# A two-block transformer kernel on one core: context work spread over the last feed-forward, retention decay arguments computed there, and another order of the expert down products

## The reference: what is computed

```
def first_block(x, ...):
    for l in range(2):
        x = x + 0.5 * swiglu(rms_norm(x, g0), ffn_w_gate[l, 0], ffn_w_up[l, 0], ffn_w_down[l, 0])   # 1024 -> 2816 -> 1024
        h = rms_norm(x, g1)
        ...                                      # three kinds of attention, gated and merged
        x = x + merged @ w_o[l]
        x = x + 0.5 * swiglu(rms_norm(x, g2), ffn_w_gate[l, 1], ffn_w_up[l, 1], ffn_w_down[l, 1])
    return rms_norm(x, final_g)

def second_block(x, c, ctx, c_ctx, ...):
    mod_x = silu(c) @ w_ada + b_ada              # shifts, scales and gates for x
    mod_c = silu(c_ctx) @ w_ada + b_ada          # the same for the context
    hx = _rmsnorm(x, norm1_g) * (1 + sc1) + sh1
    hc = _rmsnorm(ctx, norm1_g) * (1 + csc1) + csh1
    qa, ka, va, qr, kr, vr, gr = split(hx @ w_in)            # of hc: ka, va, kr, vr
    attn_x = softmax attention of x over context and x
    ret_x  = retention: scores times exp(log_g * distance), forward and backward
    x = x + gt1 * (concat(attn_x, ret_x) @ w_out)
    h2 = _rmsnorm(x, norm2_g) * (1 + sc2) + sh2
    logits = h2 @ w_router + b                   # 4 groups and 32 experts
    x = x + gt2 * (two chosen experts: (silu(h2 @ w_gate[e]) * (h2 @ w_up[e])) @ w_down[e])
    return _rmsnorm(x, final_norm_g)
```

## Time and profile before

| | |
|---|---|
| median of 3 runs | 1986.72 us (1986.06 to 1990.2) |
| the profiled execution | 1989.03 us |
| its span | 1987.1 us |
| TensorE busy | 1936.6 us (97%) |
| VectorE busy | 1236.4 us (62%) |
| ScalarE busy | 702.0 us (35%) |
| mean granted TensorE clock | 0.992 of 2.4 GHz |

### The profile page before, as it was taken

How to read it: one execution, slowest core, us unless ns; L and a number is a source line. 1 busy time by engine, 2 the same in 40 slices (tenths; PEclk the granted TensorE clock), 3 DMA queues, 4 the chain that set the end, 5 groups by cost and what they waited for, 6 DMA issues and landing times.

```text
span 1987.1 us, 33458 instructions
## 1 busy us (share of the span) xinstructions
PE 1936.6 (97%) x13957; PEld 1594.9 (80%) x13957; DVE 1236.4 (62%) x2117; ACT 702.0 (35%) x1046; POOL 40.5 (2%) x28
## 2 busy tenths in 40 slices
PE   9999999999999999999999999999899999999997
PEld 9999998889999999999888999999566444433432
DVE  7665759877567877785987777767766332222221
ACT  5433436535334533443653544343332000000001
POOL 1000100001000100010000100000000000000000
PEclk9999999999999999999999999999899999999999
DMA  8798563276776677666325675654309999999996
GB/s 246 246 357 252 176 184 114 96 212 207 220 221 203 210 233 228 201 184 185 117 96 179 204 239 185 201 121 128 127 22 369 402 421 421 421 421 422 421 421 280
DMA packets 275425, 476.64 MB, mean 240 GB/s; under 512 B 29270, under 2 KB 235152, under 8 KB 250696
## 3 DMA queue, kind: packets, MB, share of 16 engines
q1 hardware_dynamic: 275020, 474.38, 68.8%
q10 hardware_dynamic: 252, 0.08, 0.0%
HBM read 473.27 MB, written 7.95 MB: 242 GB/s over the span
## 4 chain that ended last, share of the span: by engine, by line
PE 82%; DMA 8%; DVE 6%; ACT 2%; SPq 1%; issue 1%; DVEq 0%; ACTq 0%
PE ps L793 81%; DMA ring_over<-in_moe_w_up_dram 3%; DMA ring_zone<-in_moe_w_up_dram 3%; DMA hl_place<-in_moe_w_up_dram 1%; DMA ring_over<-in_moe_w_gate_dram 1%; SPq L713 1%; PE ps L1121 1%; DVE WL L1900 1%; ACT mT L1546 0%; DVE hl L1912 0%; DVE xT L1919 0%; PE ps L1264 0%; DVE PT L2348 0%; DVE WL L1972 0%; PE ps L1441 0%
## 5 line engine op out<-in xcount | busy, mean ns | idle before, releaser
L793 PE MATMUL ps<-hh,WH 128*128 128x256 f32 x2232 | 633.3, 284 | 6.2 <-DVE WL L1900 5.6
L1900 DVE SCALAR_TENSOR_TENSOR WL<-W,WH 128x1024 fp32r<-128x1024 f32 x390 | 484.6, 1257 | 232.6 <-ACT WH L1523 231.0
L793 PE MATMUL ps<-hl,WH 128*128 128x256 f32 x2232 | 622.7, 279 | 0.0
L793 PE MATMUL ps<-hh,WL 128*128 128x256 f32 x2232 | 622.6, 279 | 0.0
L1523 ACT ACTIVATE WH<-W 128x1024 fp32r<-128x1024 f32 x390 | 408.6, 1056 | 432.9 <-PE ps L793 406.4
L793 PEld LDWEIGHTS ps<-hh,WH 128*128 128x128 f32 x2232 | 418.9, 188 | 18.1 <-issue 15.0
L793 PEld LDWEIGHTS ps<-hl,WH 128*128 128x128 f32 x2232 | 418.4, 187 | 1.2 <-issue 1.0
L793 PEld LDWEIGHTS ps<-hh,WL 128*128 128x128 f32 x2232 | 419.1, 188 | 0.0
L793 PE MATMUL ps<-hid_h,WH 128*128 128x256 f32 x704 | 200.9, 285 | 0.0
L793 PE MATMUL ps<-hid_l,WH 128*128 128x256 f32 x704 | 197.5, 280 | 0.0
L793 PE MATMUL ps<-hid_h,WL 128*128 128x256 f32 x704 | 197.4, 280 | 0.0
(11 more groups left out here) (407 smaller groups left out, 2618.0 us busy)
## 6 DMA issues: line engine op xcount, KB each, us to landing
W<-in_ffn_w_gate_dram SPq DMA_DIRECT2D x88, 512.0 KB, 4.8
W<-in_ffn_w_up_dram SPq DMA_DIRECT2D x88, 512.0 KB, 4.8
W<-in_ffn_w_down_dram SPq DMA_DIRECT2D x88, 512.0 KB, 3.8
W<-in_w_in_dram SPq DMA_DIRECT2D x78, 512.0 KB, 4.4
ring_over<-in_moe_w_gate_dram SPq DMA_DIRECT2D x29, 1024.0 KB, 25.3
ring_over<-in_moe_w_up_dram SPq DMA_DIRECT2D x28, 1024.0 KB, 24.5
W<-in_w_gate_dram SPq DMA_DIRECT2D x48, 512.0 KB, 3.5
ring_zone<-in_moe_w_down_dram SPq DMA_DIRECT2D x24, 1024.0 KB, 26.3
```

What stands on the lines that cost most here:

```text
L793: ins = nc.tensor.matmul(o, lhsT, rhs, start=start, stop=stop, skip_group_check=True, **kw)
L1900: v.scalar_tensor_tensor(out=low, in0=W[:, i % RAW, :], scalar=1.0, in1=high.bitcast(F32), op0=ALU.mult, op1=ALU.subtract).then_inc(low_re ...
```

## The change

The change has three parts.

1. The context's work in block 6 is broken up. The product of the shift and the router's weights, and VectorE's copy of its row, go to block 7 (`router_shift`, `shift_row`); the spreading matmul and `LB` go from block 7 to block 8. In block 6 VectorE and ScalarE now issue one split behind the second group of the context (`used(1)` at b == 1), and count one less at the block's end.
2. The decay arguments of the four heads are computed by VectorE at the ends of blocks 7, 8, 9 and 10 of the last feed-forward, with scratch in `QK[:, 16:18]`. In the input product only exponentials and sums are left, and `tmpD` has four tiles, one a head. ScalarE waits for argument h + 1 of `dpart`.
3. In `down_product` the second half of the chunks (j = 1) is done half of the columns by half: both chunks for columns 0 to 511, then both for 512 to 1023.

```diff
-        tmpD = flat(mT[:, :, :])[:, 0:512]
+        tmpD = [flat(mT[:, :, :])[:, h * 512:(h + 1) * 512] for h in range(4)]
+        arg_part = flat(QK[:, 16:18, :])
...
                     turns.step()
+
+            def router_shift():
+
                 bank = begin()
                 for k in range(KD):
                     mm(bank[0:1, 0:40], MOD[:, 24 + k, 0:1], WR[:, k, :], k == 0, k == KD - 1,
...
                     if (l, i, b) == (1, 1, CONTEXT_AT + 2):
+                        router_shift()
+                    if (l, i, b) == (1, 1, CONTEXT_AT + 3):
                         pe.wait_ge(lrow_ready, 1)
...
                 for j in range(2):
                     w = [take("moe_down") for e in range(2)]
-                    for c in (2 * j, 2 * j + 1):
-                        for half in range(2):
-                            at = (c % 2) * D + half * 512
-                            for e in range(2):
+                    turn = [(c, half) for c in (2 * j, 2 * j + 1) for half in range(2)]
+                    if j:
+                        turn.sort(key=lambda ch: ch[1])
+                    for c, half in turn:
+                        at = (c % 2) * D + half * 512
+                        for e in range(2):
...
                     nc.scalar.activation(hc_h[:, 2 * b:2 * b + 2, :], cT[:, 2 * b:2 * b + 2, :], ACT.Copy)\
                         .then_inc(ctx_high, 1)
                     turns.step()
+                    if b == 1:
+                        used(1)
...
                     if b:
-                        used(2)
+                        used(1 if (l, i, b) == (1, 1, CONTEXT_AT + 1) else 2)
...
-                act.wait_ge(dpart, due(dpart))
+                act.wait_ge(dpart, h + 1)
...
+            def decay_arg(h):
+
+                own = Dm[:, h, 2:4, :].rearrange("p a t -> p (a t)")
+                v.tensor_scalar(own, const("distance"), 0.0, lf[:, h:h + 1], ALU.max, ALU.mult)
+                link(v.tensor_scalar(arg_part, const("distance"), 0.0, dect[:, 4 + h:5 + h], ALU.min, ALU.mult))
+                v.tensor_tensor(own, own, arg_part, ALU.add).then_inc(dpart, 1)
+                dve.wait_ge(dpart, h + 1)
...
                         v.tensor_tensor(hc_l[:, 2 * b - 2:2 * b, :], cT[:, 2 * b - 2:2 * b, :],
                                         hc_h[:, 2 * b - 2:2 * b, :].bitcast(F32), ALU.subtract).then_inc(ctx_low, 1)
+                    if b == 1:
+                        used(1)
+
+            def shift_row():
+
                 bank = take()
                 give(v.tensor_copy(lrow[:, :], bank[0:1, 0:40]))
...
+                    if (l, i) == (1, 1) and CONTEXT_AT + 2 <= b < CONTEXT_AT + 6:
+                        decay_arg(b - CONTEXT_AT - 2)
...
                 if 0 < p - DECAY_AT <= 4:
                     decay_sum(p - DECAY_AT - 1)
-                if 0 <= p - DECAY_AT < 4:
-                    decay_arg(p - DECAY_AT)
```

More of the change, by code:

```diff
@@ L1452, in down_product @@
                     w = [take("moe_down") for e in range(2)]
-                    for c in (2 * j, 2 * j + 1):
-                        for half in range(2):
-                            at = (c % 2) * D + half * 512
-                            for e in range(2):
-                                mm(bank[half][e * SLOTS:(e + 1) * SLOTS, :], hidT[:, c, e * SLOTS:(e + 1) * SLOTS],
-                                   w[e][:, at:at + 512], c == 0, c == HIDDEN - 1,
-                                   then=work_ready if e and c == HIDDEN - 1 else None)
+                    turn = [(c, half) for c in (2 * j, 2 * j + 1) for half in range(2)]
[4 more added lines that the diff above has]
+                        for e in range(2):
+                            mm(bank[half][e * SLOTS:(e + 1) * SLOTS, :], hidT[:, c, e * SLOTS:(e + 1) * SLOTS],
+                               w[e][:, at:at + 512], c == 0, c == HIDDEN - 1,
+                               then=work_ready if e and c == HIDDEN - 1 else None)
                     done_plain(2)
@@ L1641, in ffn @@
                         round_context()
-                        turns.step()
-                    if (l, i, b) == (1, 1, CONTEXT_AT + 2):
-                        turns.step()
+                    turns.step((l, i, b) in ((1, 1, CONTEXT_AT + 2), (1, 1, CONTEXT_AT + 3)))
                     if b:
-                        used(2)
+                        used(1 if (l, i, b) == (1, 1, CONTEXT_AT + 1) else 2)
                 turns.step(ada_unit(l, i, FF_BLOCKS - 1) is not None)
@@ L1748, in decay @@
                 dist = const("distance").rearrange("p (a t) -> p a t", a=2)
-                act.wait_ge(dpart, due(dpart))
+                act.wait_ge(dpart, h + 1)
                 nc.scalar.activation(ctxd, dist, ACT.Exp, bias=lf256[:, h:h + 1], scale=lf[:, h:h + 1])
-                nc.scalar.activation(tmpD.rearrange("p (a t) -> p a t", a=2), dist, ACT.Exp,
+                nc.scalar.activation(tmpD[h].rearrange("p (a t) -> p a t", a=2), dist, ACT.Exp,
                                      bias=lf256[:, 4 + h:5 + h], scale=dect[:, 4 + h:5 + h])
@@ L2174, in ffn @@
                     if (l, i, b) == (1, 1, CONTEXT_AT + 2):
+                        shift_row()
+                    if (l, i, b) == (1, 1, CONTEXT_AT + 3):
                         bank = take()
@@ L2371, in side @@
                     both(5, 7, QK[:, 5, :])
-            def decay_arg(h):
-                own = Dm[:, h, 2:4, :].rearrange("p a t -> p (a t)")
-                v.tensor_scalar(own, const("distance"), 0.0, lf[:, h:h + 1], ALU.max, ALU.mult)
-                link(v.tensor_scalar(PT[:, 0, :], const("distance"), 0.0, dect[:, 4 + h:5 + h], ALU.min, ALU.mult))
-                v.tensor_tensor(own, own, PT[:, 0, :], ALU.add).then_inc(dpart, 1)
             def decay_sum(h):
@@ L2381, in decay_sum @@
                 ctxd = Dm[:, h, 0:2, :].rearrange("p a t -> p (a t)")
-                link(v.tensor_tensor(ctxd, ctxd, tmpD, ALU.add))
+                link(v.tensor_tensor(ctxd, ctxd, tmpD[h], ALU.add))
             for p, g in enumerate(ORDER):
```

## The result

| | before | after |
|---|---|---|
| median, runs side by side | 1988.46 us (1986.06 to 1990.56, 4 runs) | 1969.49 us (1968.79 to 1971.52, 4 runs) |
| ratio | | 0.991, 95% interval 0.9894 to 0.9926 |
| the profiled execution | 1989.03 us | 1971.52 us |
| its span | 1987.1 us | 1969.7 us |
| TensorE busy | 1936.6 us (97%) | 1927.9 us (98%) |

The time lies 0.1 us from the predicted 1969.4 us, inside the range. Part of so small a distance is luck, as the experiments show. The profiled execution became 17.5 us shorter; the sum had 17.3.

A forecast was written before the change was run, and what follows sets the result against it. TensorE, holding 82% of the chain of waits, was taken as the bound, with waits behind VectorE; loads bound the experts' stage. Savings of 5.1 + 12.0 + 0.2 = 17.3 us from 1986.7 gave 1969.4 us, range 1966.0 to 1975.5.

The forecast's parts named there:

- The fourth rival: Experts' stage: loads do not start earlier and the gain goes; no change, 1986.5 us; 3%.
- Part 1, 5.1 us: Blocks 6 and 7: removing a 4.37 us wait and half clock saves 7.1, less a new 2.0 us wait.
- the 0.45 of the sum: Block 6 check: some 0.45 us subtracted for a small modulation product that block 6 was said not to have.
- The pair count: Blocks 6 and 7: split 41 ends at 1235.0, pair 42 at 1240.3, wanted at 1238.3; new wait 2.0 us.
- Would it cost the clock too? I take no: Block 7: the new 2.0 us wait leaves the clock at 1.00, as behind step 11's 2.33 us wait.
- the bound of 2.9: Block 7: cost of a half-clock stretch if it followed the new wait, 2.9 us on top of 2.0.
- The second rival: Block 7: the new wait halves the clock; 13.4 to 14.4 us saved, about 1973 us; 17%.
- Part 2, 12.0 us: Input product: attention loop starts 11.0 us earlier, at 1404.8, plus 1.0 us from the clock staying up.
- The third rival: Input product steps 10 to 12: TensorE keeps waits of 4.5 us; 12.8 saved, 1973.9 us; 8%.
- Feed-forward cost, 0 us: Blocks 7 to 10: added arguments of 1.6 us each hide behind 6.2 us of cover; 6.4 us if uncovered.
- The fifth rival: Blocks 7 to 10: VectorE becomes the bound once block 7's free 3.6 us are used; slower, 1987.6 to 1991 us; 2%.
- Part 3, 0.2 us: Last expert pair: VectorE's read of the first half no longer lies ahead of the scatters; bounds 0 and 0.7 us.

The follow-up runs named there:

- context_only: Kernel before with only the context's edits; median 1982.58 us against 1985.82, ratio 0.998.
- down_only: Kernel before with only the order of the down products changed; median 1987.22 us against 1985.82, ratio 1.0008.
- context_again: Kernel before with only the context's edits, profiled and timed again in another batch; median 1982.86 us against 1986.93, ratio 0.9979.
- tanh_first: Kernel before with ScalarE's three exponentials of a head issued one step later, behind the Tanh; median 1982.67 us against 1986.07, ratio 0.9983.
- decay_only: Kernel before with only the decay arguments moved to blocks 7 to 10; median 1972.11 us against 1985.82, ratio 0.9933.
- arg_x3: Changed kernel with each decay argument computed three times over, same result; one execution of 1975.66 us.
- arg_x6: Changed kernel with each decay argument computed six times over, same result; 1991.56 to 1995.89 us against a median of 1986.07 before, ratio 1.0039.
- after_again: Changed kernel run and profiled once more with no edit; median 1970.97 us against 1986.93 before, ratio 0.9918.
- none_inside: Changed kernel without the split between the context's groups in block 6; median 1970.52 us against 1986.07 before, ratio 0.9921.
- two_inside: Changed kernel with one more split moved, behind the third context group; median 1969.45 us against 1985.82 before, ratio 0.9913.
- ada_late: Changed kernel with VectorE's second half of block 6's modulation sums put behind the block's splits; median 1967.66 us against 1986.93 before, ratio 0.9899.

## Why the prediction was right, and where it was not

**Bounds.** TensorE's waits were the place to look, and C and D in the table show that a gain ahead of the experts arrives whole: 17.17 us at the load behind `m_ready`, 17.71 at the last scatters. The fourth rival is out.

**Part 1, 5.1 us.** In the profile beside the one of before, the gate's read of block 8 came 5.10 us earlier, and 4.67 were left a block on, since the spreading matmul now stands in block 8 (17.83 us against 17.40). Against the 5.1 that is 0.4 too little: 0.2 by the wait (2.22 for 2.0), 0.2 by what was removed. The prediction had read this matmul wrongly: it took the 0.44 us between the blocks 7 and 8 of the kernel before for a small product of the modulation. Both blocks have one; the 0.44 is the spreading matmul. A block with neither lasts 16.97 us there (the one from 1281.35 to 1298.32), 0.43 less than the "plain" 17.40, so the 0.45 of the sum was right by luck. The pair count was good: split 41 at 1235.0, pair 42 at 1240.3. The step that failed is "Would it cost the clock too? I take no". It does in four of six profiles, and where A can be compared it costs 1.4 to 1.5 us (98.91 to 99.05 against 97.51); the bound of 2.9 was about twice that, since the low stretch is 3.4 us long each time and not 6.8. By A part 1 saves 4.7 us with the clock up and 3.1 to 3.3 with it down, and the medians of the two batches with part 1 alone gave 3.2 and 4.1 us: less than 5.1 each time. The second rival, to which I gave 17%, is thus what happens more often than the forecast, at a price so small that both lie in the range.

Why was the clock of 1.00 behind the 2.33 us at 1395 a poor guide? It was one execution of a thing that goes either way. Three more profiles have the same wait of 2.33 us. In context_only the clock stays at 1.00 behind it; in down_only (the first two rows) and context_again it does not:
```profile
1395.19 0.36 PE L793 MATMUL ps<-WH,hc_h 128*128 128x256 f32 x1 [2.33 <-DVE S L2367]
1396.00:1399.00 3.00, 3.00 (x17) 3.00 (x16) 2.11 (x4) 0.78 (x2) 0.00 (x0) 0.51 0.53 167
...
1393.28 0.55 PE L793 MATMUL ps<-WH,hc_h 128*128 128x256 f32 x1 [2.33 <-DVE S L2377]
1393.00:1398.00 5.00, 4.72 (x22) 4.75 (x23) 3.14 (x6) 1.69 (x3) 0.00 (x0) 0.50 0.46 153
```
It cost nothing there: B is 94.12 to 94.14 us in all four, as TensorE waits there for VectorE anyway. The Trainium skill ("TensorE: Matmul & The Clock Gate", "A second HAM failure mode") tells of short idles that come often between groups of matmuls and throttle again. The wait of 2.22 us stands alone, so it goes beyond what that section describes.

**Part 2, 12.0 us.** 11.28 at the loop's start against 11.0, 12.50 at the load behind against 12.0: the clock and the first rounds gave 1.22 us where I took 1.0. That term hangs on the execution before: against the other profiles without part 2 it is 0.6 to 1.5. Removing the last feed-forward's gain of 4.67, the loop starts at 1404.55 against 1404.8. Its two halves are shown apart by tanh_first. The third rival (waits stay in steps 10 to 12) is out: TensorE has none there.

**Feed-forward cost, 0 us.** Right: pairs 47 and 48 were split by 1254.4 and pair 49 by 1257.3, all ahead of my count, and decay_only has no new wait. The fifth rival named the wrong point: I wrote that it decides when the free 3.6 us of block 7 are used up. arg_x3 adds 3.3 us on top of the 1.6, and no split is late. The lead of three pairs, 6.2 us, covers it, as the prediction counted; at the last block the residual sums behind the argument decide. Whether arg_x6 lost its time by that lead or by VectorE's work exceeding a whole block is not separated.

**Part 3, 0.2 us.** It is 0. VectorE's read did leave the path, but it had never been on it: the scatters need TensorE itself, which is busy until the last down matmul in either order.

**The median.** The paired medians give 19.0 us here and 16.0 in after_again's batch, around the traces' 17.2 to 17.7. The hit to 0.1 us is a fair sum on a lucky draw.

## What to carry to other kernels

Reordering alone did not remove the wait here. When an engine is late as a whole, a split put elsewhere only moves the wait (none_inside, two_inside); ask instead which work ahead of it has no reader yet, and put that behind, as ada_late does. Work may be hidden in a stage as long as each piece is shorter than the lead of what is queued behind it and the engine's whole work still fits into the stage (4.9 us a block did, 9.6 did not), and the last piece must be checked against what follows the stage. And compare kernels by lengths between fixed instructions: here they repeat to 0.03 us where the clock stays up (B with part 2: 82.85 to 82.88) and whole executions of the kernel before differ by 7. Where the clock may fall, as in A, one profile is one draw.

## What the runs showed of the hardware

- One program with one and the same TensorE wait of 2.22 to 2.23 us had a granted clock of 1.00 behind it in one profile and 0.53 in the next. A clock read from one profile is one draw.
- The same goes for the wait of 2.33 us in step 11: 1.00 behind it in before and context_only, half in down_only (3.4 us long) and context_again (6.8 us). Waits of 0.27, 0.73 and 0.74 us had 1.00 behind them.
- The half clock behind the wait of 2.22 to 2.23 us lasted 3.4 us in all four profiles where it fell, and cost 1.4 to 1.5 us in the three that can be compared. Behind the wait of 4.37 us it lasted 6.8 us in three profiles and 3.4 in down_only.
- The last down product of 32 matmuls took either 7.09 or 8.78 us, 1.69 us apart, with no difference in the program (8.78 in after, 7.09 in after_again); in the longer cases a stretch of 3.4 us at half clock lies in it.
- The start of block 6 varied from 1217.86 to 1220.90 us between kernels that do the same work until then.
